# Moving the first gather into the mixing stage and the shared expert's down products into the expert loop

## The reference

```
p   = x @ W_in
s   = HalfGLU(S5_bidir(p_ssm));  a = MLA(p_q, p_kv)
x1  = LN(alpha * x + [s ; a] @ W_o)
# 64 routed experts, top 6 per token, and one shared expert of the same width (256)
routed = sum over the 6 picked experts e of  w[token, e] * (silu(x1 @ Wg[e]) * (x1 @ Wu[e])) @ Wd[e]
shared = (silu(x1 @ ws_gate) * (x1 @ ws_up)) @ ws_down
out = LN(alpha * x1 + routed + shared)
```

## Time and profile before

| | |
|---|---|
| median of 3 runs | 1488.89 us (1487.53 to 1491.71) |
| the profiled execution | 1491.52 us, span 1489.7 us |
| TensorE busy | 1411.3 us, 95% of the span |
| VectorE, ScalarE, GpSimd busy | 791.8, 372.9, 613.5 us |
| mean granted clock of TensorE | 0.987 |
| DMA moved | 322.16 MB, mean 216 GB/s |
| expert stage (from L1688 on) | 707.17 us to the end of the span |

### The profile page before, as it was taken

How to read it: one execution, slowest core, us unless ns; L and a number is a source line. 1 busy time by engine, 2 the same in 40 slices (tenths; PEclk the granted TensorE clock), 3 DMA queues, 4 the chain that set the end, 5 groups by cost and what they waited for, 6 DMA issues and landing times.

```text
span 1489.7 us, 17006 instructions
## 1 busy us (share of the span) xinstructions
PE 1411.3 (95%) x5242; PEld 723.6 (49%) x5242; DVE 791.8 (53%) x1410; ACT 372.9 (25%) x742; POOL 613.5 (41%) x590
## 2 busy tenths in 40 slices
PE   7999999999997999998899999999999999999976
PEld 3444666666665455553344444444444444444432
DVE  3575999999986148883333333333333333333326
ACT  0314656665555122210101010010010010010005
POOL 0008445666500003342655555555555555555520
PEclk9999999999998999999999999999999999999998
DMA  9506100100133700051999999999999999999945
GB/s 235 83 29 76 19 15 13 19 18 14 43 101 113 293 32 30 29 206 54 355 357 374 363 374 370 363 373 370 363 373 373 362 371 368 362 370 370 317 76 226
DMA packets 116410, 322.16 MB, mean 216 GB/s; under 512 B 46470, under 2 KB 66590, under 8 KB 91394
## 3 DMA queue, kind: packets, MB, share of 16 engines
q1 hardware_dynamic: 92946, 261.99, 47.9%
q0 software_dynamic: 23408, 59.45, 16.4%
HBM read 276.45 MB, written 51.72 MB: 220 GB/s over the span
## 4 chain that ended last, share of the span: by engine, by line
DMA 43%; PE 4%; issue 3%; DVE 1%; POOL 1%; POOLq 0%; ACT 0%; SPq 0%; DVEq 0%
DMA sum_d<-moe_y,moe_idx 41%; PE moe_p_gu L1729 2%; DMA moe_xg<-x_d,moe_idx 1%; PE moe_p_y L1749 1%; DMA mixers_ring_b<-sum_d 0%; DVE all_x_sb L1976 0%; DVE all_x_sb L1969 0%; POOL moe_xg L1674 0%; PE moe_p_y L1797 0%; DVE moe_y L1909 0%; PE moe_p_s L1804 0%; POOL moe_xg L1688 0%; POOLq L1670 0%; DVE moe_xgT L1892 0%; PE moe_p_gu L1804 0%
## 5 line engine op out<-in xcount | busy, mean ns | idle before, releaser
L1674 POOL DMA_INDIRECT moe_xg<-x_d,moe_idx x260 | 263.7, 1014 | 115.2 <-issue 58.9
L1749 PE MATMUL moe_p_y<-mixers_ring_b,moe_hT 128*128 128x512 f32 x520 | 233.9, 592 | 0.9 <-DVE moe_hT L1903 0.9
L1729 PE MATMUL moe_p_gu<-mixers_ring_b,moe_xgT 128*128 128x512 f32 x512 | 225.0, 592 | 0.0
L1892 DVE STREAM_TRANSPOSE moe_xgT<-moe_xg 128x1024 f32<-128x1024 f32 x65 | 131.8, 2028 | 171.2 <-DMA moe_xg<-x_d,moe_idx 171.2
L1685 POOL DMA_INDIRECT sum_d<-moe_y,moe_idx x65 | 105.8, 1627 | 240.7 <-DMA sum_d<-moe_y,moe_idx 188.2
L1909 DVE TENSOR_SCALAR moe_y<-moe_p_y,shared_block_w 128x512 f32<-128x512 f32 x65 | 48.8, 751 | 223.2 <-DMA sum_d<-moe_y,moe_idx 180.2
L1749 PEld LDWEIGHTS moe_p_y<-mixers_ring_b,moe_hT 128*128 128x128 f32 x520 | 98.7, 190 | 125.0 <-issue 123.9
L1729 PEld LDWEIGHTS moe_p_gu<-mixers_ring_b,moe_xgT 128*128 128x128 f32 x512 | 95.1, 191 | 107.1 <-issue 107.1
L1245 POOL DMA_INDIRECT slot_d<-all_entry,all_dest_i x48 | 48.4, 1007 | 224.0 <-DVE all_dest_i L1491 211.8
L1830 ACT ACTIVATE moe_y<-moe_p_y,shared_block_w 128x512 f32<-128x512 f32 x65 | 44.7, 688 | 352.6 <-DMA sum_d<-moe_y,moe_idx 327.8
L1729 PE MATMUL moe_p_gu<-mixers_ring_a,moe_xgT 128*128 128x512 f32 x272 | 121.3, 599 | 3.9 <-DVE moe_xgT L1892 3.9
(11 more groups left out here) (361 smaller groups left out, 1948.2 us busy)
## 6 DMA issues: line engine op xcount, KB each, us to landing
mixers_ring_b<-in_we_down_dram SPq DMA_DIRECT2D x65, 1024.0 KB, 16.9
mixers_ring_b<-in_we_gate_dram SPq DMA_DIRECT2D x32, 1024.0 KB, 14.8
mixers_ring_b<-in_we_up_dram SPq DMA_DIRECT2D x32, 1024.0 KB, 23.2
mixers_ring_a<-in_we_gate_dram SPq DMA_DIRECT2D x17, 1024.0 KB, 13.6
mixers_ring_a<-in_we_up_dram SPq DMA_DIRECT2D x17, 1024.0 KB, 22.7
mixers_o<-in_we_gate_dram SPq DMA_DIRECT2D x16, 1024.0 KB, 15.0
mixers_o<-in_we_up_dram SPq DMA_DIRECT2D x16, 1024.0 KB, 22.5
moe_xg<-x_d,moe_idx POOLq DMA_INDIRECT x260, 8.3
```

The costliest lines, as they stand in the source:

```text
L1674: nc.gpsimd.indirect_dma_start(xg[:, u, g, :], None, x1_quarters, bass.IndirectOffsetOnAxis(ap=idx[:, c, g:g + 1], axis=0), bounds_check=N ...
L1729: last = nc.tensor.matmul(p_gu[:, u, :], xgT[:, u, kk, :], k.moe_gu[v][:, :, kk * F:(kk + 1) * F], start=(kk == 0), stop=(kk == KD - 1))
L1749: last = nc.tensor.matmul(p_y[:, half * 512:(half + 1) * 512], hT[:, u, kk, :], k.moe_dn[v][:, kk * D + half * 512:kk * D + (half + 1) * 512],
L1892: nc.vector.transpose(xgT[:, u].rearrange("p k (g i) -> p g k i", g=NQ), xg[:, seat].rearrange("p g (j k) -> p g k j", k=KD)).then_inc(x_t ...
```

## The change

1. The seats `xg` and their semaphores are made before the mixing stage (they hold that stage's `g1`, `b1` and `r` first). GpSimd zeroes them behind the scatters of tile 5, SP writes 8 zero tiles to `sum_d` from seat 0, and GpSimd gathers block 0 at the end of the mixing stage, straight from `block_idx`. The stores of x1 share one semaphore, on which that gather waits.
2. TensorE runs the last part of the shared gate and up products behind the transposes that make the table. Weight slot 2 and the down weights of slots 2 and 3 are loaded in the mixing stage (`x1T` is laid out by halves for this); gain and bias are loaded late.
3. The expert stage starts with gathers 1 and 2; one copy of five index rows replaces the first five copies.
4. The shared down products go into the loop: 16 pieces (8 tiles, two halves), one behind `down` in every fourth `step`. ScalarE copies the tile of `s_hT` that a piece needs (`pick_tile`), VectorE adds the piece to alpha x `k.x` (`add_shared`) between `keep_y` and `keep_hT`. `k.x` stays on the chip.
5. At the end TensorE adds both by identity products, for all 8 tiles: `k.x` (`take(t, k.x, True)`) and the loaded sums (`take(t, sums, False)`), and every tile is normed from PSUM.

```diff
             for e in range(2):
                 load_expert(sp, k, e, e)
             load_gate_up(sp, k, RING - 1, RING - 1)
+            sp.wait_ge(wiped, 1)
+            for t in range(T):
+                sp.dma_start(k.sum_d[t * P:(t + 1) * P, :], k.xg[:, 0].rearrange("p g w -> p (g w)")).then_inc(sum_wiped, 16)
             sp.wait_ge(where_done, 1)
...
-            for t in range(T):
-                sp.wait_ge(x1_out[t], 16)
+            sp.wait_ge(gu_done, 2)
+            load_gate_up(sp, k, 2, 2)
+            sp.wait_ge(gu_done, 4)
+            for e in range(2, RING):
+                load_down(sp, k, e, e)
...
                 scatter(t)
+                if t == T - 3:
+                    pool.wait_ge(x1_done, T)
+                    nc.gpsimd.memset(k.xg[:, :, :, :], 0.0).then_inc(wiped, 1)
...
+            pool.wait_ge(x1_out, 16 * T)
+            pool.wait_ge(sum_wiped, 16 * T)
+            pool.wait_ge(idx_made, 1)
+            for g in range(NQ):
+                nc.gpsimd.indirect_dma_start(k.xg[:, 0, g, :], None, k.x1_quarters,
...
-            for n in range(2, 4):
-                for part in range(2):
-                    shared(n, part)
+            shared(2, 0)
+            shared(2, 1)
+            shared(3, 0)
...
             last.then_inc(table_turned, 1)
+            shared(3, 1)
...
-            load_expert(sp, k, 2, 2)
-            load_down(sp, k, RING - 1, RING - 1)
-            sp.dma_start(g2[:, :], k.ln2_g.to_broadcast([P, D])).then_inc(ln_in, 16)
-            sp.dma_start(b2[:, :], k.ln2_b.to_broadcast([P, D])).then_inc(ln_in, 16)
-            for t in range(T):
...
-                sp.dma_start(k.sum_d[t * P:(t + 1) * P, :], k.x[:, t, :]).then_inc(sum_out, 16)
...
-            nc.gpsimd.memset(xg[:, :, :, :], 0.0).then_inc(wiped, 1)
-            pool.wait_ge(wiped, 1)
-            for e in range(SEATS):
-                gather(e, OVER + e, e, e)
-            gather(3, OVER + 3, 0, 3, free=1)
-            gather(4, OVER + 4, 1, 4, free=2)
-            pool.wait_ge(sum_out, 16 * T)
+            gather_listed(1)
+            gather_listed(2)
+            nc.gpsimd.tensor_copy(idx[:, 0:LISTED, :], k.block_idx[:, OVER:OVER + LISTED, :]).then_inc(idx_done, 1)
+            pool.wait_ge(idx_done, 1)
+            gather_listed(3, free=1)
+            gather_listed(4, free=2)
             scatter(0, 0, 0, first=True)
...
-            def step(n, c, first=False):
+            def shared_down(half, piece):
+                cols = slice(half * 512, (half + 1) * 512)
+                if piece is not None:
+                    pe.wait_ge(s_read, piece)
+                    pe.wait_ge(s_picked, piece)
+                for f in range(KF):
+                    lhsT = s_tile[:, f, :] if piece is not None else k.s_hT[:, f, 0:P]
+                    last = nc.tensor.matmul(p_s[:, half, :], lhsT, k.ws_dn[:, f, cols],
+                                            start=(f == 0), stop=(f == KF - 1))
+                last.then_inc(s_done, 1)
+
+            def step(n, c, first=False, shared=None):
 
                 gate_up(n, c + 1)
                 down(n, c, first)
+                if shared is not None:
+                    shared_down(*shared)
                 turn_h(n, c + 1)
...
+            step(0, 1, shared=(0, None))
+            with pe.Fori(0, T - 1) as n:
                 for v in range(RING):
-                    step(n, v + 2)
+                    step(n, v + 2, shared=(0, n + 1) if v == RING - 1 else None)
+            with pe.Fori(T - 1, 2 * T - 1) as n:
+                for v in range(RING):
+                    step(n, v + 2, shared=(1, n + 1) if v == RING - 1 else None)
...
+            def take(t, tile, first):
                 for half in range(2):
                     cols = slice(half * 512, (half + 1) * 512)
...
+                    last = nc.tensor.matmul(rows[t % 4][:, cols], k.ident, tile[:, t, cols], start=first, stop=not first)
+                return last
+
+            pe.wait_ge(s_read, 2 * T)
+            pe.wait_ge(y_dve, n_over + E)
+            pe.wait_ge(y_act, n_over + E)
+            for t in range(4):
+                take(t, k.x, True)
+            for t in range(T):
                 pe.wait_ge(sum_in[t], 16)
...
+                take(t, sums, False).then_inc(r_done, 1)
+                if t + 4 < T:
+                    pe.wait_ge(r_read, t + 1)
+                    take(t + 4, k.x, True)
...
+            def pick_tile(tile, piece):
+                act.wait_ge(s_done, piece)
+                nc.scalar.activation(s_tile[:, :, :], k.s_hT[:, :, bass.ds(tile * P, P)], ACT.Copy).then_inc(s_picked, 1)
...
             for t in range(T):
-                if t < EARLY:
-                    act.wait_ge(sum_in[t], 16)
-                else:
-                    act.wait_ge(r_done, t - EARLY + 1)
+                act.wait_ge(r_done, t + 1)
...
+            def add_shared(tile, half, piece):
+                dve.wait_ge(s_done, piece + 1)
+                x_half = x_halves[:, bass.ds(tile * 2 + half, 1), :].rearrange("p o w -> p (o w)")
+                nc.vector.scalar_tensor_tensor(x_half, x_half, ALPHA, p_s[:, half, :], ALU.mult, ALU.add).then_inc(s_read, 1)
...
-                if t >= EARLY:
-                    dve.sem_inc(r_read, 1)
+                ch.link(nc.vector.scalar_tensor_tensor(k.x[:, t, :], rows[t % 4], nmean[:, t:t + 1], g2[:, :], ALU.add, ALU.mult))
+                dve.sem_inc(r_read, 1)
```

More of the change, by code:

```diff
@@ L1141, in mix_norm_route @@
         r_bias = sb("r_bias", [P, N_EXPERTS], f32)
-        g1 = sb("g1", [P, D], f32)
-        b1 = sb("b1", [P, D], f32)
+        g1, b1, r = [k.xg[:, u].rearrange("p g w -> p (g w)") for u in range(SEATS)]
         oT = sb("oT", [P, 2, 4, P], f32)
-        r = sb("r", [P, D], f32)
         stats = sb("stats", [P, 2, 6], f32)
@@ L1189, in mix_norm_route @@
         main_in, spread_done, table_turned = sem("main_in"), sem("spread_done"), sem("table_turned")
-        x1_out = [sem(f"x1_out{t}") for t in range(T)]
+        x1_out = sem("x1_out")
+        wiped, sum_wiped, idx_made = sem("wiped"), sem("sum_wiped"), sem("idx_made")
         x_back = [sem(f"x_back{t}") for t in range(T)]
@@ L1303, in route @@
                 for kk in range(KD):
-                    last = nc.tensor.matmul(p_log, k.x1T[:, kk, t * P:(t + 1) * P], w_r[:, kk, :], start=(kk == 0), stop=(kk == KD - 1))
+                    last = nc.tensor.matmul(p_log, k.x1T[:, t // 4, kk, t % 4 * P:(t % 4 + 1) * P], w_r[:, kk, :], start=(kk == 0), stop=(kk == KD - 1))
                 last.then_inc(logits, 1)
@@ L1589, in moe_experts @@
         rows = [p[:, :, :].rearrange("p h n -> p (h n)") for p in (p_s, p_gu, p_pair)] + [p_y[:, :]]
-        xg_in = [sem(f"xg_in{u}") for u in range(SEATS)]
+        x_halves = k.x[:, :, :].rearrange("p t (h w) -> p (t h) w", h=2)
         y_out = sem("y_out")
@@ L1830, in keep_y @@
                 nc.scalar.activation(y[:, u, 0:512], p_y[:, 0:512], ACT.Copy, scale=k.block_w[:, bass.ds(col, 1)]).then_inc(y_act, 1)
-            for t in range(EARLY, T):
-                nc.scalar.activation(k.x[:, t, :], k.x[:, t, :], ACT.Copy, scale=ALPHA).then_inc(grown, 1)
+            def pick_tile(tile, piece):
+                act.wait_ge(s_done, piece)
+                nc.scalar.activation(s_tile[:, :, :], k.s_hT[:, :, bass.ds(tile * P, P)], ACT.Copy).then_inc(s_picked, 1)
             gate(0, 0)
@@ L1838, in _, with four @@
             keep_y(1, 1, OVER + 1, sent=False)
-            with act.Fori(0, E // 4 - 1) as ii:
+            def four(ii, tile):
                 for v in range(4):
@@ L1842, in _ @@
                     gate(i + 1, (v + 1) % 2)
+                    if v == 0:
+                        pick_tile(tile, ii + 1)
                     keep_y(i, v % 2, ii * 4 + (OVER + 2 + v))
+            with act.Fori(0, T - 1) as ii:
+                four(ii, ii + 1)
+            with act.Fori(T - 1, 2 * T - 1) as ii:
+                four(ii, ii - (T - 1))
             gate(E - 1, 1)
@@ L1862, in square @@
                 act.wait_ge(mean_done, t + 1)
-                nc.scalar.activation(junk[:, :], row(t), ACT.Square, bias=nmean[:, t:t + 1],
+                nc.scalar.activation(junk[:, :], rows[t % 4], ACT.Square, bias=nmean[:, t:t + 1],
                                      accum_out=tot[:, 1, t:t + 1]).then_inc(squared, 1)
@@ L1870, in _ @@
             for t in range(T):
-                if t < EARLY:
-                    act.wait_ge(sum_in[t], 16)
-                else:
-                    act.wait_ge(r_done, t - EARLY + 1)
+                act.wait_ge(r_done, t + 1)
                 if t:
                     act.wait_ge(squared, t)
-                nc.scalar.activation(junk[:, :], row(t), ACT.Copy, accum_out=tot[:, 0, t:t + 1]).then_inc(added, 1)
+                nc.scalar.activation(junk[:, :], rows[t % 4], ACT.Copy, accum_out=tot[:, 0, t:t + 1]).then_inc(added, 1)
                 act.wait_ge(added, t + 1)
@@ L1925, in _, with twelve @@
```

(23 more changed lines are left out.)

87 lines of the change are left out of this document (30 added, 57 removed).

## The result

The changed kernel took 1515.3 us (median of 4 runs, 1514.48 to 1518.04) against 1488.3 us before (4 runs): ratio 1.0184, 95% interval 1.017 to 1.0197. It is 1.8% slower. The forecast was 1505.8, with a range of 1492 to 1518. The profiled execution took 1514.89 us, of which the span is 1512.9, 23.2 more than the span before.

A forecast was written before the change was run, and what follows sets the result against it. The prediction took a serial chain of scatter DMAs, with the DMA engines full, to bound the expert loop. Start -10.4, loop -0.9 and end +28.2 give +16.9 us, on the median of 1488.9 1505.8 us, range 1492 to 1518.

The forecast's parts named there:

- Start: Up to the first scatter: earlier table and early gather 0 save time, -10.4 us, bounds -8 and -13.
- The 2.2 us of barrier: Between mixing and expert stages: the barrier takes 2.2 us as before, so the stage starts at 709.0.
- The 6.1 us from gather 1's last issue to its turn: Start of the expert stage: gather 1, last issued at 713.8, lands 6.1 us later, at 719.9.
- the bound of -13: Start: the most it could save, -13 us, with entries on time and landings of 4 us.
- Loop: First to last scatter: added pieces hide in TensorE's slack, sum -0.9 us, bounds -8 and +5.
- the -1.4 for the first two intervals: Loop's first two scatter intervals, 12.11 and 11.64 before: shorter with 9 MB of other traffic gone, -1.4 us.
- The margin: Loop: TensorE's step with pieces takes 10.96 us against a scatter interval of 11.17, margin 0.2 us.
- End: After the last scatter: tiles 0 to 4 come slower, +28.2 us, bounds +18.6 and +34.9.
- the ring: End: next tile's sums stand behind the wait for r_read, so each turn takes 10.3 us, four turns 41.2.
- The end that costs nothing: Rival, end: TensorE's wait is covered and tiles follow every 2.9 us, total 1476.2; chance 0.07.
- The clock that stays up: Rival, end: TensorE keeps its full clock in the bursts, +18.6 us, total 1496.2; chance 0.12.
- TensorE as the bound: Rival, loop: TensorE becomes the bound, fully exposed pieces cost 27.5 us, total 1533; chance 0.07.

The follow-up runs named there:

- before_again: The kernel before the change, unchanged, run once more for a second profile; 1488.82 us (one execution).
- downs_late: x_early with the down weights of slots 2 and 3 issued behind the barrier instead of at the mixing stage's end; 1485.13 us, ratio 0.9975.
- gather_late: tail_order with gather 0 moved back behind the barrier; 1490.88 us, ratio 1.0017.
- no_pieces: tail_order without the shared down products, their copies and additions, and without the product of x1 and alpha; 1482.89 us, ratio 0.9958.
- scatter_first: tail_order with scatter 0 issued ahead of gather 4; 1485.09 us, ratio 0.9979.
- double_pieces: tail_order with each piece's four products done twice, same result; 1507.53 us, ratio 1.0121.
- tail_order: The changed kernel with the end's sums of tiles 0 to 3 no longer behind a wait for r_read; 1486.41 us, ratio 0.9981.
- warm_fill: The changed kernel with 8 zero-matrix instructions on TensorE ahead of each wait for r_read at the end; 1507.54 us, ratio 1.013.

## Why the prediction was right, point by point

**Start: right, by misses that cancelled and by some luck.** -10.60 against -10.4. Against before_again it would have been -7.4, and from the mark in the ranks it is -9.3 to -9.5, so that the agreement within 0.2 us is luck, while a gain of 7 to 10 us is borne out. The entries came at 695.3 (forecast 696.6) and the index stood at 698.4 (699.3). The 2.2 us of barrier were the step that failed: they were counted from VectorE's last product, while with an early gather the barrier's end follows that gather (7.6 us after its last issue). It came 3.9 us after VectorE's last product, and the stage began at 710.84 instead of 709.0. The 6.1 us from gather 1's last issue to its turn were the other: they were 2.3. The row of 6.1 had been taken with 9 MB in flight (DMA share 0.98 at 382 GB/s from 715 to 721); the 2.3 were taken with little traffic (0.20 at 57 GB/s from 715.5 to 717.9). That it is the traffic which makes it long, downs_late bears out: with 2 MB of weights issued beside gather 1 (0.78 at 303 GB/s from 715 to 721) it took 5.2. The landings of 4 us in the bound of -13 were my estimate, and no run shows them: where VectorE waited for a gather at the start of the stage, its turn came 2.1 to 2.4, 5.2, or 6.0 to 6.8 us after the last issue. The short landing did not make the start shorter, since block 0's products, started late, were last instead. That the early gather brings most of it was shown by gather_late (6.0 of 9.5).

**Loop: sign wrong, size small.** +2.35 against -0.9. That the pieces hide in TensorE's slack was right: no_pieces shortens the chain of scatters by 0.15 us. The step that failed is the -1.4 for the first two intervals: they were 12.44 and 11.79 (12.11 and 11.64 before), though the 9 MB were gone. Gather 4 ahead of scatter 0 isn't why (scatter_first). What makes the first intervals long, and why the loop up to the 60th scatter is some 2 us longer even without the pieces (662.55 against 660.6 and 660.8), stays open. The margin was as thin as forecast: double_pieces is past it.

**End: mechanism right, size low.** +31.45 against +28.2. tail_order takes the ring away and with it 29 us. Two terms were mis-sized. Tile 0 was to come 1.9 us later; it came 3.7 later (13.87 us from the last scatter against 10.16), because TensorE adds x of four tiles first, starts them only 2.5 us after the last scatter's issue, the first four instructions at 3.75 us (granted clock 0.50 from 1441.1 to 1445.0) where four take 1.88 at the full clock (1450.66, granted 1.00), and is still at it when the sums land. I had called TensorE warm there. The turns were 10.7 on average, forecast 10.3; one of them, the 12.23 from tile 1 to tile 2, holds a load of ScalarE's table of 1.28 us (at 1463.18), which I had left out. The clock's part was in the forecast (6.0 for the 8 instructions, measured 5.3 to 6.7 in the four turns, 6.1 on average), and warm_fill shows it apart: 9.6 us of the 42.7 in the profiles, 7.8 in the medians. The granted clock was 0.67 with TensorE idle 4.27 us at each wait (1470 to 1490 after), and 1.00 with it idle 0.84 (1470 to 1484 in warm_fill).

**Sum.** The three parts of the span miss by 0.2, 3.3 and 3.3 us, together 6.3 too low. The other 3.2 of the 9.5 us between 1505.8 and 1515.3 are no mechanism of the change: the sum was put on a median 2.6 us under the profiled execution of before (1491.52), while the profiled execution of after (1514.89) lies at its median.

**Rivals.** The end that costs nothing (1476.2): fell; the turn was 10.7, not under 5. The clock that stays up (1496.2): fell, the rows show 6.3 us where 3.7 would be. TensorE as the bound (1533): fell.

## What to carry to other kernels

When work goes from one in-order queue into another, write down the queue's order and ask of each wait what stands behind it that is already able to run; here a few lines in another order were worth 29 us, more than all that the change won. A slack of 0.2 us in 11 could be spent, but not overspent: past it, at a step of 11.39 us against an interval of 11.17, the loop took 11.5 us more and the end of the loop another 10.8, because the engine's lead was gone. A gather issued just ahead of a barrier of all engines lost part of its head start here to a longer barrier, which ended 3.9 us after VectorE's last product instead of 2.2. And before two profiles are set against each other, look for a mark ahead of the change: here the stages ahead of it moved by 3 us from one profile to the next of the same kernel.
